# Four of a sequence's eight value pages at another place of GpSimd's queue: a hybrid decoder step on one core

## The reference, cut to what matters

```python
xn = rmsnorm(x, norm_mix)
... = split_projection(xn, w_in)                  # queries, keys, values, gates of both mixers
o_nsa  = gates * (compressed, selected, window attention)   # 8 heads, 2 groups
o_diff = rmsnorm(diff_attention(q, k_all, v_all)) # 4 heads, two softmax maps each
x = x + (gate_nsa * (o_nsa @ w_br_nsa) + gate_diff * (o_diff @ w_br_diff)) @ w_out
x = x + moe_ffn(rmsnorm(x, norm_ffn))             # 32 experts, top 4, clamped SwiGLU
```

## Time and profile before

| | |
|---|---|
| median of three runs | 1422.0 us |
| the profiled execution | 1418.69 us, its span 1417.0 us |
| TensorE busy | 1378.5 us (97%) |
| VectorE, ScalarE, GpSimd busy | 467.3, 285.8, 98.0 us |
| DMA | 509.39 MB, mean 359 GB/s |
| chain that ended last | PE 74%, DMA 17%, DVE 3% of the span |

### The profile page before, as it was taken

How to read it: one execution, slowest core, us unless ns; L and a number is a source line. 1 busy time by engine, 2 the same in 40 slices (tenths; PEclk the granted TensorE clock), 3 DMA queues, 4 the chain that set the end, 5 groups by cost and what they waited for, 6 DMA issues and landing times.

```text
span 1417.0 us, 19616 instructions
## 1 busy us (share of the span) xinstructions
PE 1378.5 (97%) x7363; PEld 603.9 (43%) x7363; DVE 467.3 (33%) x1024; ACT 285.8 (20%) x611; POOL 98.0 (7%) x218
## 2 busy tenths in 40 slices
PE   9999999999999999999999999999999999999987
PEld 4445556777753543333333333333333333333322
DVE  1115484665436442313312223132221331321314
ACT  3004434555540301110010110100100111011002
POOL 1000223534200000000000000000000000000000
PEclk9999999999999999999999999999999999999999
DMA  7335857989988699999999999999999999999996
GB/s 273 119 118 192 285 135 239 328 282 315 356 265 308 260 426 383 422 429 428 428 428 428 429 429 428 428 429 429 428 428 429 429 428 429 429 428 429 429 428 247
DMA packets 75484, 509.39 MB, mean 359 GB/s; under 512 B 19082, under 2 KB 25714, under 8 KB 46098
## 3 DMA queue, kind: packets, MB, share of 16 engines
q1 hardware_dynamic: 61394, 477.88, 82.9%
q0 software_dynamic: 13184, 27.82, 6.1%
q10 hardware_dynamic: 864, 3.15, 0.6%
HBM read 502.29 MB, written 10.62 MB: 362 GB/s over the span
## 4 chain that ended last, share of the span: by engine, by line
PE 74%; DMA 17%; DVE 3%; issue 2%; ACT 2%; SPq 1%; DVEq 0%; POOL 0%; POOLq 0%; ACTq 0%
PE PS L1487 25%; PE PS L1517 11%; DMA arena<-in_w_gate_up 10%; PE PS L1457 6%; PE PS L364 5%; DMA arena<-in_w_down 5%; PE PS L2194 4%; PE PS L1449 4%; PE PS L614 3%; PE PS L600 3%; PE PS L1345 2%; DMA arena<-in_cache_diff_k 2%; PE PS L373 1%; PE PS L2164 1%; PE PS L1504 1%
## 5 line engine op out<-in xcount | busy, mean ns | idle before, releaser
L1487 PE MATMUL PS<-arena 128*64 128x512 f32 x2048 | 455.8, 595 | 13.1 <-DMA arena<-in_w_gate_up 12.2
L1487 PEld LDWEIGHTS PS<-arena 128*64 128x64 f32 x2048 | 141.8, 137 | 294.4 <-issue 264.6
L1517 PE MATMUL PS<-arena 128*64 128x512 f32 x1024 | 227.0, 594 | 2.3 <-DMA arena<-in_w_down 2.2
L1949 DVE TENSOR_SCALAR arena<-PS 128x512 f32<-128x512 f32 x32 | 22.1, 692 | 444.3 <-PE PS L1496 443.3
L1517 PEld LDWEIGHTS PS<-arena 128*64 128x64 f32 x1024 | 71.7, 137 | 150.1 <-issue 143.8
L1457 PE MATMUL PS<-arena 128*128 128x512 f32 (+1 forms) x180 | 84.2, 608 | 0.0
L1449 PE MATMUL PS<-arena 128*128 128x512 f32 (+1 forms) x192 | 79.4, 618 | 4.5 <-ACT arena L1657 3.7
L1868 DVE TENSOR_TENSOR arena<-PS,arena 128x512 f32<-128x512 f32 x32 | 21.8, 686 | 167.7 <-PE PS L1465 166.7
L364 PE MATMUL PS<-arena 128*128 128x512 f32 (+1 forms) x192 | 77.0, 561 | 0.0
L1306 POOL COPY arena<-arena 96x64 bf16 (+1 forms) x34 | 7.9, 234 | 988.0 <-PE PS L1524 942.5
L1642 ACT ACTIVATE arena<-arena 128x512 f32<-128x512 f32 x32 | 20.1, 630 | 267.2 <-DVE arena L1949 267.2
(11 more groups left out here) (294 smaller groups left out, 1274.9 us busy)
## 6 DMA issues: line engine op xcount, KB each, us to landing
arena<-in_w_gate_up SPq DMA_DIRECT2D x128, 2048.0 KB, 20.1
arena<-in_w_down SPq DMA_DIRECT2D x62, 2048.0 KB, 21.9
arena<-in_w_in SPq DMA_DIRECT2D x8, 2048.0 KB, 13.0
arena<-in_cache_diff_k SPq DMA_DIRECT2D x64, 256.0 KB, 5.9
arena<-in_cache_diff_v POOLq DMA_DIRECT2D x64, 256.0 KB, 5.0
arena<-in_cache_cmp_kv POOLq DMA_DIRECT2D x64, 128.0 KB, 3.9
arena<-in_cache_sel_kv SPq DMA_DIRECT2D x64, 128.0 KB, 6.9
arena<-in_w_out SPq DMA_DIRECT2D x1, 4096.0 KB, 14.3
```

Source lines behind the costliest of these rows:

```text
L1487: last = nc.tensor.matmul(bank(2 + role + 2 * u)[64 * h:64 * h + 64], hTm[:, k, BS * u:BS * u + BS], rows[:, D * role + 512 * h:D * role + ...
L1517: last = nc.tensor.matmul(bank(6 + u)[64 * h:64 * h + 64], aT[u][:, c % 4, 64 * (c // 4):64 * (c // 4) + 64], down_w[u][c // 4][:, c % 4, ...
L1949: st(V.tensor_scalar(g1, bank(2 + 2 * u), LIM, None, ALU.min), g1_ready)
```

## The change

`values_in` takes the range of pages that it issues. In `next_turn`, which serves turns 1 to 3, sequence 0's first four value pages are issued where all eight were. The other four are issued after the compression pages of the next turn's sequence 0 and after a new wait on the transposes of `kd0` of this turn. In turn 3 there is no next turn, so only the new wait stands between the halves. Turn 0 is not touched.

```diff
-            def values_in(pages, i, b, first=False):
-                for pg, page in enumerate(pages):
+            def values_in(pages, i, b, first=False, part=range(NPAGE)):
+                for pg in part:
+                    page = pages[pg]
                     if pg == 0 and not first:
                         past(pool, l_pv, i * VALUES + ((PV_D1 if b else PV_D0) - VALUES))
                     pool.dma_start(in_runs(dv_raw[b], pg // RUN, pg % RUN), page_runs(vd_d, page)).then_inc(dv_in[2 * b + pg // 4], 16)
...
                 cmp_pages(pool, pages[1], i, 1, range(4, NPAGE))
-                values_in(pages[0], i, 0)
+                values_in(pages[0], i, 0, part=range(NPAGE // 2))
                 if not last:
                     cmp_pages(pool, pages_of(POOL, i + 1, 0), i + 1, 0)
+                past(pool, l_tp, i * L_TP + (NPAGE + group_at("kd0", last) + 1))
+                values_in(pages[0], i, 0, part=range(NPAGE // 2, NPAGE))
                 past(pool, l_tp, i * L_TP + (NPAGE + group_at("pd2", last) + 1))
                 values_in(pages[1], i, 1)
```

## The result

The changed kernel takes 1431.03 us (median of six runs, 1425.84 to 1434.16); the kernel before took 1421.99 (six runs, 1418.49 to 1424.06). The ratio is 1.0065 with a 95% interval of 1.0047 to 1.0083: slower by about 9 us. The forecast was 1422.4 and no change, and the range ended at 1426.5.

The account below looks back on a forecast made before the run. Attention bound by TensorE, DMA engines close behind. Turns 1 to 3 at +0.4, -0.3 and +0.3 us sum to +0.4, so the median goes from 1422.0 to 1422.4 us; range 1418.0 to 1426.5.

Parts of the forecast that it names:

- The waits at `kd0`: TensorE's waits for key pages in turns 1 to 3: all three gone as keys land sooner, -1.51 us.
- Nothing lost at the moved pages, at GpSimd's queue, at the selected pages: Moved pages in time by 1.8 to 4.3 us, 2.3 us of issue hidden, selected pages with 2.5 us slack: no cost.
- Who is last: Sequence 1's values end the busy stretch, slack 0.19 and 0.64 us, turn 3 waiting 1.74: only 0.64 us of gain kept.
- What the move does to the end of the stretch: Sequence 1's values land later by what the DMA engines idle: 0.6, 0.3 and 0.3 us in turns 1 to 3.
- the keys' long flight: Last key page's 7.15 us from issue to landing in turn 1, read as deep queues and so little idling.
- handed back with a surplus: Rival: engines idle the full 2.5 us, each turn's last value pages land that much later; +6.3 us, 1428.3; chance 0.13.
- The rule on the queues: Transfers from different issuing engines share 16 DMA engines, so the moved megabyte costs 2.5 us anywhere; sum near zero.
- The bound of 2.5 us: Upper limit on how much later the end of a turn's busy DMA stretch comes, the moved pages' time at full rate.
- After the attention: Nothing there depends on the DMA queues' history; a shift of the turns' end moves the rest one to one.
- The measure of what can be told: A difference under 0.3% (4.3 us) in the kernel's time can't be told from none.
- the chance of 0.10 for slower: Chance that the kernel's time rises by over 0.3% (4.3 us), mostly from the surplus rival; no change had 0.85.

Follow-up runs that it names:

- last_turn_only: Turns 1 and 2 as in the kernel before, only turn 3 split with the new wait on kd0; 1426.91 us, 1.0039 of the kernel before.
- last_turn_branch_later: last_turn_only with SyncE's second branch weights and the gates behind them held until sequence 1's value product is done; 1426.16 us, 1.0044 of the kernel before.
- left_out: Changed kernel with sequence 0's second four value pages neither loaded nor waited for in turns 1 to 3; 1422.60 us, 1.0016 of the kernel before.
- left_out_again: left_out unchanged, run once for a second profile; 1421.4 us.
- half_on_sync: Changed kernel with the second four pages in SyncE's queue, their own semaphore and no wait on kd0; 1434.79 us, 1.0103 of the kernel before.
- order_only: Changed kernel without its new wait on kd0; 1427.53 us, 1.0044 of the kernel before.
- kd7_after: Changed kernel with sequence 1's value pages issued behind kd7 instead of pd2; 1430.22 us, 1.0062 of the kernel before.
- before_again: The kernel before, unchanged, run once for a second profile; 1421.0 us.

## Why the prediction was wrong

**The waits at `kd0`.** Right: 0.40, 0.45 and 0.66 us are gone. This was the whole of the gain.

**Nothing lost at the moved pages, at GpSimd's queue, at the selected pages.** Right. The first product never waited; no copy of VectorE stretched GpSimd's issues (2.27 us for four); the new wait was met in turns 1 and 2; `sel3` had no wait.

**Who is last.** Right in kind: the step named sequence 1's values as the transfers that had 0.19 and 0.64 us of slack and would take the gain, and the wait stands there.

**What the move does to the end of the stretch: the step that failed.** The prediction put it at "0.6 us in turn 1, 0.3 in turn 2 and 0.3 in turn 3, nearer to the lower end", between bounds of 0 and 2.5 us. Turn 1 measured 2.6 us, the whole of the upper bound, turn 2 3.7, and the four turns of two pairs of profiles 3.3 in the mean. The reason given for the low end was the keys' long flight, which "needs something in front of them". But what had stood in front of them was the moved half. With it gone nothing took its place: in the trace compression pages are issued at 276, the window at 276, selected pages at 275. 1.0 of 1.05 MB was missing by 284. The rows needed were read; the mistake was to price a hole by how full the engines were with the thing that was being taken away. The shares of 0.92 and 0.96 were even read both ways, as nearly full where the gain was priced and as spare room where the loss was. The rival "handed back with a surplus" had the right place, and gave 1428.3; its +6.3 us were too little too, as the waits on values grew by 11.0.

**The rule on the queues.** The prediction let the sum come out near zero by the rule of the Trainium skill, "DMA: Bandwidth & Descriptors", under "Issuing engines are not separate DMA queues". That rule is on which engine issues, not on when: it doesn't say that a later issue costs nothing. A megabyte issued later cost 0.88 or 0.49% here.

**Turn 3.** The bound of 2.5 us was not a bound. The wait grew by 4.9 us in the profile (8.5 in last_turn_only), as the delayed pages are then in flight with weights (last_turn_branch_later, 2.83 us of wait without them).

**The clock.** It had no term. A wait of some 3 us was followed by matmuls at the lower clock in most cases, which added 3.5 us to the profiled difference.

**After the attention** the step of one to one nearly held: the scores behind turn 3's products start at 403.13 before and 415.10 changed, 12.0 us of the 12.8.

**The measure of what can be told** (0.3%) was coarser than needed, as the interval of the result is 0.18% to either side; and the chance of 0.10 for slower too small: a term with bounds of 0 and +6.3 us had been placed near its end of no effect on one argument.

**Open.** Why the last page is late by more than the 2.5 us of the moved bytes, and why left_out, with less to move, still waits. In left_out the mean DMA share is below 1 while landing times grow, which would fit engines loaded unevenly, each page waiting for its slowest; a share by engine isn't in the views, so this is argued and not shown.

## What to carry to other kernels

When transfers run full up to a deadline, price a move of bytes from before the busy stretch into its middle at their whole time at least, put on whatever is last in it, and look up what each queue could issue into the hole at that moment. (Whether other work in the hole would win the time back, no run here shows.) Issue order among the queues bought nothing here: values issued 10 us earlier landed 0.7 us earlier, and pages taken out of the queue in front didn't help. And a wait in TensorE of some 3 us should be priced with the low clock behind it.

## What the runs showed of the hardware

- The granted clock fell to 0.50, the lower of its two levels, behind each of the waits of 3.14 us and more in front of the value products (64 matmuls in 3.15 to 3.64 us instead of 1.95). Of the waits of 2 to 3 us some had it and some did not: 2.13, 2.24 and 2.83 us (left_out_again, half_on_sync, last_turn_branch_later) were followed by 3.36, 3.05 and 3.41 us, while 2.18, 2.49, 2.63 and 2.98 us (order_only, kd7_after, before_again, turn 1 of the changed kernel) left 1.95 or 1.96. So the length of the wait alone doesn't tell. On eight matmuls of 128x512 it cost 2.7 us (6.32 against 3.60).
- Full engines move very different amounts: 423 GB/s at a share of 1.02 from 296 to 304 us of the changed kernel, with key and value pages (256 KB) in flight, and 278 at 1.06 from 284 to 296, with selected and compression pages (128 KB) among them. The second figure scatters: 302 in before_again at the same share.
- The last page of a group can land later than its neighbours: in turn 3 of the changed kernel the last two took 8.4 and 12.8 us, in turn 1 of the kernel before 4.8 and 6.1.
